# Seven half products for the first two column chunks of the last projection of a two-layer encoder step

## The reference, cut to what matters

```python
def trunk(x, ...):                       # 512 prompt rows and 8 x 16 sample rows, D_MODEL 2048
    x = layer_a(x, ...)                  # state-space branch and memory attention, w_in_a, w_glu, w_out_a
    kv = rms_norm(x, g_kv) @ w_kv        # 2048 x 3072, shared keys and values
    x = layer_b(x, kv, ...)

def layer_b(x, k_all, v_all, ...):
    hn = rms_norm(x, g_pre)
    q, gate, mq, mg = _split_proj(hn @ w_in)                                  # 2048 x 4096
    o = stick_breaking_attention(q, k_all, v_all, q_offset)
    b_out = o * jax.nn.silu(gate)
    m_out = mem_attention(mq, mk, mv) * jax.nn.silu(mg)
    out = jnp.concatenate([b_out, m_out], axis=-1) @ w_out                    # 2048 x 2048
    return x + rms_norm(out, g_post)
```

## Time and profile before

| | |
|---|---|
| median of 3 runs | 2183.7 us (2182.33 to 2185.88) |
| profiled execution, its own time | 2181.02 us |
| its span | 2179.2 us |
| TensorE busy | 2146.1 us of the span, 98% |
| DVE, ACT, POOL busy | 1265.5, 930.3, 332.9 us |
| DMA | 343.86 MB, mean 158 GB/s |

### The profile page before, as it was taken

How to read it: one execution, slowest core, us unless ns; L and a number is a source line. 1 busy time by engine, 2 the same in 40 slices (tenths; PEclk the granted TensorE clock), 3 DMA queues, 4 the chain that set the end, 5 groups by cost and what they waited for, 6 DMA issues and landing times.

```text
span 2179.2 us, 33578 instructions
## 1 busy us (share of the span) xinstructions
PE 2146.1 (98%) x12428; PEld 1841.3 (84%) x12428; DVE 1265.5 (58%) x2098; ACT 930.3 (43%) x1753; POOL 332.9 (15%) x498
## 2 busy tenths in 40 slices
PE   8999999999999999999999999999999999999998
PEld 6788888888888998888788887888888888988887
DVE  5758889888744446544654545455555554663223
ACT  4643332333355343222534444556565654552221
POOL 1532202211101001111100000222222222010000
PEclk9999999999999999999999999999999999999999
DMA  7744434443745337885344666544444445444224
GB/s 256 238 117 106 113 109 112 116 110 106 218 139 170 110 107 246 282 272 203 127 178 135 211 195 211 156 153 135 140 136 151 136 140 192 162 142 174 77 77 155
DMA packets 194928, 343.86 MB, mean 158 GB/s; under 512 B 26740, under 2 KB 106272, under 8 KB 190112
## 3 DMA queue, kind: packets, MB, share of 16 engines
q1 hardware_dynamic: 142576, 181.35, 27.3%
q0 software_dynamic: 31104, 121.23, 17.4%
q10 hardware_dynamic: 21168, 40.18, 5.6%
HBM read 276.65 MB, written 65.39 MB: 157 GB/s over the span
## 4 chain that ended last, share of the span: by engine, by line
PE 80%; DVE 12%; issue 3%; ACT 3%; DMA 2%; DVEq 0%; ACTq 0%; SPq 0%; POOL 0%
PE PS L231 13%; PE PS L232 12%; PE PS L233 12%; PE PS L1609 8%; PE PS L1611 8%; PE PS L1610 8%; DVE WL L213 2%; PE PS L1571 2%; PE PS L1573 2%; PE PS L1572 2%; PE PS L845 1%; DVE FA L676 1%; DVE FA L672 1%; DVE FA L667 1%; DVE FA L669 1%
## 5 line engine op out<-in xcount | busy, mean ns | idle before, releaser
L231 PE MATMUL PS<-XH,WH 128*128 128x512 f32 (+1 forms) x1408 | 522.7, 371 | 1.7 <-DVE EST L2580 1.7
L232 PE MATMUL PS<-XL,WH 128*128 128x512 f32 (+1 forms) x1408 | 511.1, 363 | 0.0
L233 PE MATMUL PS<-XH,WL 128*128 128x512 f32 (+1 forms) x1408 | 510.4, 363 | 0.0
L213 DVE SCALAR_TENSOR_TENSOR WL<-RAW,vec,WH 128x256 fp32r<-128x256 f32 (+1 forms) x608 | 281.5, 522 | 307.4 <-ACT WH L198 302.8
L198 ACT ACTIVATE WH<-RAW,vec 128x256 fp32r<-128x256 f32 (+1 forms) x608 | 282.3, 534 | 244.5 <-DMA RAW<-in_w_kv_dram 98.3
L208 DVE TENSOR_TENSOR WL<-RAW,WH 128x1024 fp32r<-128x1024 f32 (+1 forms) x152 | 181.7, 1197 | 335.4 <-ACT WH L194 334.9
L1609 PE MATMUL PS<-WH,XH 128*128 128x512 f32 x848 | 333.2, 393 | 6.9 <-DVE WL L213 4.5
L1610 PE MATMUL PS<-WL,XH 128*128 128x512 f32 x848 | 330.8, 390 | 0.0
L1611 PE MATMUL PS<-WH,XL 128*128 128x512 f32 x848 | 330.7, 390 | 0.0
L194 ACT ACTIVATE WH<-RAW 128x1024 fp32r<-128x1024 f32 (+1 forms) x152 | 155.7, 1026 | 368.3 <-DMA RAW<-in_w_out_b_dram 129.7
L233 PEld LDWEIGHTS PS<-XH,WL 128*128 128x128 f32 x1408 | 264.4, 188 | 38.1
(11 more groups left out here) (363 smaller groups left out, 3003.1 us busy)
## 6 DMA issues: line engine op xcount, KB each, us to landing
RAW<-in_w_in_a_dram SPq DMA_DIRECT2D x64, 512.0 KB, 4.1
RAW<-in_w_in_b_dram SPq DMA_DIRECT2D x64, 512.0 KB, 4.4
RAW<-in_w_kv_dram SPq DMA_DIRECT2D x48, 512.0 KB, 4.1
RAW<-in_w_out_a_dram SPq DMA_DIRECT2D x32, 512.0 KB, 5.2
FA<-in_w_kv_dram POOLq DMA_DIRECT2D x16, 1024.0 KB, 7.7
RAW<-in_w_out_b_dram SPq DMA_DIRECT2D x32, 512.0 KB, 3.8
scratch_in_a<-EST ACTq DMA_DIRECT2D x32, 320.0 KB, 3.4
RAW<-in_w_glu_dram SPq DMA_DIRECT2D x24, 384.0 KB, 3.3
```

The source lines that it names most:

```text
L213: ins = eng.scalar_tensor_tensor(out=wview(WL, slot, ph)[:, kt, :], in0=wview(RAW, slot, ph)[:, kt, :], scalar=vec[:, g:g + 1], in1=wview( ...
L231: pe.matmul(acc, wh, xh, start=first, stop=False, **kw)
L232: pe.matmul(acc, wh, xl, start=False, stop=False, **kw)
L233: return pe.matmul(acc, wl, xh, start=False, stop=last, **kw)
```

## The change

The first two column chunks of out_b get the treatment of the pairs: a new phase `pair_b` of 32 units in the order `OUT_UNITS`, and out_b keeps its last two chunks. Of the 32 units only T3 alternates with B12, and B22 stands last. The combined quarters of `w_out_b` are made while the pairs of the keys and values run: 16 half pieces (256 columns wide, `HALF_PIECE`), each two POOL loads of 256 KB, four DVE operations (`combine_half`, at the steps `COMBINE_KV`) and a POOL store of 512 KB to free parts of scratch tensors. The row sums of the last projection's left side are made on DVE and ACT in the first steps of `pair_b` (`set_sum_b`, `set_high_b`, `set_low_b`); the fourth set lies in columns of the output rows that are not written yet (`S4H`, `S4L` in `OUTR`). The output rows move over the branch blocks (`OUTROW_B`), the gains come in two halves, and the loads of the residual tiles wait for units of out_b.

```diff
+OUT_UNITS = [(op, g) for op in ("B11", "B21", "T2", "T1") for g in range(4)]
+OUT_UNITS += [(op, g) for g in range(4) for op in ("T3", "B12")] + [(op, g) for op in ("T4", "B22") for g in range(4)]
+SET_HIGH_AT, SET_LOW_AT = (4, 5, 6, 9), (5, 6, 7, 10)
+COMBINE_KV = [4 * x + 3 for x in range(2 * HALF_K)]
...
-                ("out_b", io["w_out_b"][0], 2, RW, None, 4, 8)):
+                ("pair_b", io["w_out_b"][0], 2, RW, None, 1, len(OUT_UNITS)),
+                ("out_b", io["w_out_b"][0], 2, RW, None, 2, 8)):
...
+        OUTROW_B, = place([(NT, D)], at=FN - NT * D)
+        S4H, S4L = OUTR[:, 0:2, D // 2:], OUTR[:, 2:4, D // 2:]
...
SP
+            for k, (op, g) in enumerate(OUT_UNITS):
+                if op[0] == "T":
+                    src = combined_b(2 * g, 2)[:, :, COMBINED.index(op), :]
+                else:
+                    src = src_wide(ph.w, g + (0 if op[1] == "1" else HALF_K // 2), 2, (int(op[2]) - 1) * RW, RW)
+                load_unit(sp, ph, ph.first + k, k, src)
...
DVE, among the pairs of the keys and values
+            def combine_half(x):
+                b11, b12, b21, b22 = (HALF_PIECE[x % 2][:, j, :] for j in range(4))
+                dve.wait_ge(s_resd[x % 2], PIECES_MOVED + (16 if x % 2 else 32) + 48 * (x // 2) + 32)
+                mine(tt(b22, b22, b12, ALU.subtract))
+                mine(tt(b12, b11, b12, ALU.subtract))
+                mine.wait()
+                mine(tt(b11, b11, b22, ALU.add))
+                mine.wait()
+                tt(b21, b21, b11, ALU.subtract).then_inc(s_dg, 1)
...
                 for k in range(ph.upc):
                     ahead(split_low, dve, ph, pair_unit(pair, k), k)
+                    if ph.upc * pair + k in COMBINE_KV:
+                        combine_half(COMBINE_KV.index(ph.upc * pair + k))
...
DVE, at the start of pair_b
-            for x in range(10, KT):
+            for x in range(10, 12):
                 fill_low(dve, F_B, x, ORDER_B[x])
+            for k in range(ph.upc):
+                ahead(split_low, dve, ph, ph.first + k, k)
+                if k < 2:
+                    for x in range(12 + 2 * k, 14 + 2 * k):
+                        fill_low(dve, F_B, x, ORDER_B[x])
+                elif k < 6:
+                    set_sum_b((0, 1, 3, 2)[k - 2])
+                if k in SET_LOW_AT:
+                    n = SET_LOW_AT.index(k)
+                    set_low_b((1, 0, 3, 2)[n], n)
...
POOL, after the stores of x1
+            def load_half(x):
+                for r in range(2):
+                    pool.dma_start(HALF_PIECE[h][:, 2 * r:2 * r + 2, :], src[r][:, 0:2]).then_inc(s_resd[h], 16)
+            def store_half(x):
+                pool.wait_ge(s_dg, NT + x + 1)
+                pool.dma_start(combined_b(kt)[:, 0, :, h * CW:h * CW + CW], HALF_PIECE[h]).then_inc(s_resd[h], 16)
+            load_half(0)
+            load_half(1)
+            for x in range(2 * HALF_K):
+                store_half(x)
+                if x + 2 < 2 * HALF_K:
+                    load_half(x + 2)
+            for k in range(2):
+                pool.wait_ge(s_resd[k], PIECES_MOVED + (16 if k else 32) + HALVES_MOVED)
             mem_load(pool, 1, 0)
...
POOL, during the last projection
-            pool.dma_start(GB[:], io["g_post_b"].broadcast_to([P, D])).then_inc(s_gb, 16)
+            pool.wait_ge(s_gm, M_B + 4)
+            pool.dma_start(GB_1, io["g_post_b"][:, 0:D // 2].broadcast_to([P, D // 2])).then_inc(s_gb, 16)
+            pool.wait_ge(s_wu, phases["pair_b"].first + 24)
+            pool.dma_start(GB_2, io["g_post_b"][:, D // 2:].broadcast_to([P, D // 2])).then_inc(s_gb, 16)
             for t in range(NRES):
-                pool.dma_start(RES[t], scr["x1"][P * t:P * t + P, :]).then_inc(s_resd[t], 16)
+                pool.wait_ge(s_wu, phases["out_b"].first + 3 * t)
+                pool.dma_start(RES_B[t], scr["x1"][P * t:P * t + P, :]).then_inc(s_resd[t], 16)
```

More of the change, by code:

```diff
@@ L1945, in _ @@
+            out_products()
+            free_at = (8, 9, 7, 7, 10)
+            row_chunks(phases["out_b"], None, lambda t: pe.wait_ge(s_ev["out_b"], free_at[t]), last=1)
+            last_chunk(phases["out_b"], base=E_B)
         @block.scalar
@@ L2287, in _, with state, square @@
             layer_wait(act, 1, "gated", NT)
-            act.wait_ge(s_wu, phases["out_b"].first)
+            act.wait_ge(s_wu, phases["pair_b"].first)
             for x in ORDER_B[10:]:
                 fill_high(act, F_B, x)
+            osq, banks = s_osq[1], pair_banks(0)
+            def state(dst, bank):
+                act.activation(dst, PS[:, bank, :], ACT.Copy).then_inc(osq, 1)
+            def square(o, t, c, done):
+                act.wait_ge(osq, done)
+                act.activation(JUNK2_B, o, ACT.Square, scale=ROOT_D, accum_out=SS4_B[:, t, c:c + 1]).then_inc(osq, 1)
@@ new lines, in pair_rows_end @@
+            def pair_rows_end(k):
+                if k == 0:
+                    dve.wait_ge(s_wu, phases["out_b"].first)
+                    for i in range(2):
+                        tt(block(i, 1), block(i, 1), PS[:, banks["D"][i], :], ALU.add).then_inc(ev, 1)
+                    dve.wait_ge(osq, 14)
+                    tt(block(NT - 1, 1), PS[:, 7, :], gains_at(1, 1), ALU.mult).then_inc(ev, 1)
+                else:
+                    for i in range(2):
+                        dve.wait_ge(osq, 15 + i)
+                        scaled(i, 1)
@@ L2650, in _, with load_gate_block @@
                 pool.wait_ge(s_st["in_a"][m], 256)
[L2651 removed]
+            def load_gate_block(kb):
                 if kb >= 2:
```

268 lines of the change are left out of this document (239 added, 29 removed).

## The result

The changed kernel takes 2191.34 us (median of 9 runs, 2188.78 to 2197.03) against 2183.7 us before (median of 9 runs): ratio 1.0037, 95% interval 1.0027 to 1.0047. It is 7.6 us slower, 2.3 us above the range that I gave. One execution of all in this document, of the seventh experiment, took 3569.5 us at a granted clock of 0.556 and is left out of every figure. The changed kernel's profiled execution has a span of 2189.6 us, 10.4 us more than before; that of before lay 2.7 us under its own median, which is nearly the difference between 7.6 and 10.4.

A forecast was written before the change was run, and what follows sets the result against it. TensorE was taken as the bound: matmul count times 0.225 us, plus few waits for weights. Terms -10.8 + 2.0 + 1.1 + 4.0 = -3.7 us took 2183.7 to 2180.0 us, range 2174 to 2189.

The forecast's parts named there:

- Matmuls: In pair_b, 432 matmuls instead of 480, 48 fewer at 0.225 us each: -10.8 us, called certain.
- Start of pair_b: At unit 2 of pair_b, TensorE waits for a split behind ACT's six fills: +1.1 us.
- The alternation: Where T3 and B12 alternate in pair_b, short units cover loads too little, at units 20 and 24: +2.0 us, bounds 1.8 and 4.5.
- Residual and gains: The four 1 MB loads at out_b's start go to later units of 6.75 us with 20 us of cover: 0.
- The pieces: Among the pairs, piece DMAs delay deciding weight loads to 4.7 us landing, mainly at B22(2) and T4(0): +4.0 us, bounds 0 and 7.5.
- DVE's combining: Among the pairs, four operations of about 0.42 us, 1.7 us behind every fourth split, fit DVE's time: hidden.
- POOL's queue: After the 16th store, POOL goes on at 1372 to 1374, with 16.7 us of slack before the query rows: 0.
- Rival 1: Among the pairs, pieces are hidden and landings stay at 3.7 to 4.2 us: -7.2 us, 2176.5 us; chance 0.28.
- Rival 2: DMA engines bound the T and B22 stretches, landings about 6.3 us, all T units late: +5.9 us, 2189.6 us; chance 0.12.

The follow-up runs named there:

- seventh experiment: Changed kernel with only pair_b's second gains load at unit 29 instead of 24 and ACT's split of unit 2 after two of six fills: 2188.26 us, ratio 1.0028.
- the ninth: Changed kernel with eight pieces combined before the pairs, four at each pair's first steps, some piece loads held, pair_b's order, fills and gains moved: 2186.95 us, ratio 1.0024.
- fourth: Changed kernel with pair_b's B12 out of the alternation with T3, three between B21 units and the fourth before T4: 2193.89 us, ratio 1.0046.
- twelfth kernel: Changed kernel with four pieces combined before the pairs, six in each, loads of pieces 8, 9, 14, 15 held, pair_b's order, fills and gains moved: 2183.62 us, ratio 1.0005.
- second: Changed kernel with all piece DMAs kept but DVE's four combine_half operations on one column instead of 256: 2187.36 us, ratio 1.0022.
- eighth: Changed kernel with ACT's three stores of a pair issued at step 15 instead of 9, in both pairs: 2195.08 us, ratio 1.0044.
- tenth: Changed kernel with POOL's loads of pieces 3 and 11 held until unit 12 of their pair: 2187.70 us, ratio 1.0022.

## Why the prediction was wrong

**Matmuls, -10.8: right.** 48 fewer, at the pitch that I used, except that pair_b's undisturbed excess is 1.9 where the 480 matmuls before had 0.9: 1 us more that stood in no term.

**Start of pair_b, +1.1: right** in place and size (1.13 us at unit 2), and with the fills moved it was gone.

**The alternation, +2.0, bounds 1.8 and 4.5: inside its bounds** in the changed kernel, 2.9, and a little under them in the seventh, 1.5. Place half right: I had units 20 and 24; units 20 and 22 waited. Putting B12 elsewhere took these waits away.

**Residual and gains, 0: right for the residual, wrong for the gains, 2.0 us.** The four loads of residual tiles are issued in out_b (the first at 2073.75, when pair_b's last matmul had begun at 2073.1), and TensorE waits nowhere in out_b. But the gains' two loads of 512 KB are issued in pair_b, at 1995.29 and 2043.93. I named only the first, for a possible 1 us at units 9 to 11, where nothing waited; the second, behind unit 24, is in no term, and it met T4(3)'s load (7.6 us). I looked where the big loads go, not at every load that the change moves among short units. Issued at unit 29 it cost nothing.

**The pieces, +4.0, bounds 0 and 7.5: this step failed.** It measured 15.5 in the profiled execution, and by the medians 12.8 for the pieces in all. The median landing was nearly as I took it (4.7 said, 5.0 to 5.3 found). The error was to price the term with one landing for all deciding loads and to call the T units safe ("is late only when a collision and ACT's copies meet, 0.4"). A four-slot ring does not pay for the median but for each single load over its cover. The loads that cost most took 9.2 us (T1(1), with three stores of ACT and a piece's load beside it, engines at 0.96), and holding the piece's load alone took that wait away. The largest single loss of a pair thus lay at a unit to which I had given next to nothing. By place: at B22 and T4 TensorE waited 7.2 us in the two pairs, where the sum had 3.6; at the T1 units it lost 7.8 us (waits of 3.3, 0.5 and 2.3 and 1.7 of slow pitch), where the sum had 0.8. Both sizes were off, the T units' by far the more. My upper bound used 5.7 us, from a median again. And the slow pitch behind the long wait stood in no term. The mean share of the engines was no better guide: I had added it up to 0.91, and the three queues of the stretch make 0.76 (49.0, 21.8 and 5.6%), with loads of 9.2 us all the same.

The Trainium skill, "DMA: Bandwidth & Descriptors", section "Issuing engines are not separate DMA queues", has DMAs of scalar, sync and gpsimd interleave on the same 16 engines; the changed kernel's trace agrees (the load of 9.2 us beside the stores of ACT's queue and the load of POOL's, 5.6 us with POOL's held).

**DVE's combining, hidden: right.** 0.42 us an operation as estimated (0.419 to 0.425 us), and alone it leaves the pairs at 3.5. What I did not count is that DVE also waits for the piece; in the changed kernel, at four units apart, it never idled ahead of `combine_half` in the pairs; in pair 1 of the ninth that wait is the bound.

**POOL's queue, 0: right in cost, wrong in time.** The first key rows came at 1386.72, not 1372 to 1376, because the pairs ended 14.2 us later and the last pieces with them. POOL still waited 12.73 us for the query rows (its load at 1405.55, in place of 1391.14 after 16.68 us in the earlier trace rows), and TensorE did not wait there.

**The rivals.** Rival 1 (hidden) fell: landings rose. Rival 2 gave 2189.6 us and the slower side, and 2191.3 came. Its cause is half right. The engines are the resource, but at 0.76 to 0.84 over the windows of the pairs, not at 1.00, and not with landings of 6.3 us at all T units: it is single loads, the longest of 8.5 and 9.2 us, in stretches that fill the engines for some 10 us. That its time was the nearest of all is in part luck: it had 13.6 us for the pieces and nothing for the gains or the slow pitch. I gave it 0.12 because I asked whether the engines would be full on the mean.

**What stays open.** What DMAs and combining cost together beyond their sum (1.6 us by the medians, within their uncertainty; 5.5 by the excess): the untouched pairs of the fourth and seventh kernels repeat the changed kernel's excess to 1.1 us (18.3 and 18.5 for 19.4), so it is likely real, but no run shows how it comes about. And whether the remaining 6.5 us in the pairs of the twelfth kernel would go with more pieces placed as in pair 2 of the ninth, or outside the pairs, which wasn't tried. Executions of one kernel spread over 4 to 12 us, and much of that lies ahead of the pairs: their first matmul comes at 1162.4 to 1168.7 in the six profiled kernels that are the same up to there (changed, second, fourth, seventh, eighth, tenth). pair_b repeats less well than the pairs: 5.3 in the tenth kernel and 9.5 in the eighth for the changed kernel's 8.3, with no edit in it.

## What to carry to other kernels

When background transfers are added beside a ring of weight slots, don't price them with the median landing and the mean share of the engines: list every transfer of the other queues that can be issued within a landing of each deciding load, and take the landing of the fullest stretch there. 10.8 us of matmuls were bought here with 16.8 MB through engines that were already at 0.62, and where the pieces, the short units, the fills and the gains' load were placed decided between 7.6 us lost and level, with the same matmuls. In one pair four pieces cost nothing, where they ran beside the longer units and were there before they were asked for. Before moving such work earlier, count the turn of its own buffers as well, since an engine that waits for a piece holds up the splits behind it.
